# Order of the x and z column chunks in a hybrid decoder layer's input projection

## The reference, cut to what matters

```python
proj = rmsnorm(h, norm1_w) @ w_in               # q, k, v, z, xbc, dt, ga, gs
xbc = silu(causal_dwconv(xbc, conv_w, conv_b))  # 4 taps over positions; xs: 2048 columns, b and c: 512 each
y = ssd_chunked(xs, dt, a_log, bm, cm, d_skip)
y = y * silu(z)                                  # z: 2048 columns
yg = group_norm(y, 4 groups) * ssd_norm_w
h = h + ((gate_a * (attn @ w_attn_o) + gate_s * (yg @ w_ssd_o)) @ w_out)
```

## Time and profile before

| what | value |
| --- | --- |
| median of 3 runs | 1051.18 us |
| the runs | 1048.21, 1051.68, 1051.18 us |
| the profiled execution | 1048.02 us |
| its span, first to last instruction | 1046.3 us |
| PE busy | 1020.7 us (98%), 4991 matmuls |
| VectorE busy | 637.7 us (61%) |
| ScalarE busy | 467.2 us (45%) |
| GpSimd busy | 99.4 us (9%) |
| mean granted TensorE clock | 0.997 |

### The profile page before, as it was taken

One profiled execution on the slowest core, in us unless ns is written; L12 is line 12 of the kernel. 1 busy time (PEld: TensorE's weight loads), 2 busy tenths in 40 slices (PEclk: granted clock), 3 DMA queues, 4 the chain that ended last, 5 costly groups with the idle time before them and its releaser, 6 DMA issues.

```text
span 1046.3 us, 13313 instructions
## 1 busy us (share of the span) xinstructions
PE 1020.7 (98%) x4991; PEld 833.2 (80%) x4991; DVE 637.7 (61%) x915; ACT 467.2 (45%) x859; POOL 99.4 (9%) x132
## 2 busy tenths in 40 slices
PE   6999999999999989999999999999999999999997
PEld 6877777777888778778888888898888888888886
DVE  4537998795475685795663543557666666651323
ACT  6235656453555544557652322445443444431132
POOL 3001111110222110112230110000000000000000
PEclk9999999999999999999999999999999999999999
DMA  7622122224556333454444643132323223232212
GB/s 227 127 86 81 56 67 81 81 81 121 148 126 170 93 110 102 130 141 142 121 137 155 222 151 131 54 108 81 108 92 120 80 80 114 74 134 99 91 71 81
DMA packets 123641, 117.01 MB, mean 112 GB/s; under 512 B 21357, under 2 KB 111797, under 8 KB 123589
## 3 DMA queue, kind: packets, MB, share of 16 engines
q1 hardware_dynamic: 95653, 95.26, 29.4%
q10 hardware_dynamic: 25344, 12.59, 5.2%
q0 software_dynamic: 2592, 8.46, 2.3%
HBM read 109.93 MB, written 6.36 MB: 111 GB/s over the span
## 4 chain that ended last, share of the span: by engine, by line
PE 76%; DVE 12%; issue 7%; ACT 3%; POOL 1%; DMA 1%; ACTq 0%; DVEq 0%; SPq 0%; POOLq 0%
PE banks L1175 24%; PE banks L1177 23%; PE banks L1176 23%; DVE w_lo L830 2%; DVE conv_acc L1123 2%; PE banks L1273 1%; ACT decay L651 1%; PE banks L1221 1%; PE banks L1241 1%; ACT probs L608 1%; DMA x_nat<-in_x 1%; PE banks L1188 1%; DVE small L906 1%; DVE scores L903 1%; PE banks L1261 0%
## 5 line engine op out<-in xcount | busy, mean ns | idle before, releaser
L830 DVE TENSOR_TENSOR w_lo<-w_raw,w_hi 128x1024 fp32r<-128x1024 f32 (+1 forms) x166 | 199.6, 1242 | 112.1 <-ACT w_hi L574 110.7
L574 ACT ACTIVATE w_hi<-w_raw 128x1024 fp32r<-128x1024 f32 (+1 forms) x170 | 166.7, 1029 | 112.4 <-PE banks L1177 107.6
L1175 PE MATMUL banks<-xn_hi,w_hi 128*128 128x512 f32 x528 | 212.9, 403 | 0.7 <-DVE w_lo L830 0.5
L1176 PE MATMUL banks<-xn_lo,w_hi 128*128 128x512 f32 x528 | 206.7, 391 | 0.0
L1177 PE MATMUL banks<-xn_hi,w_lo 128*128 128x512 f32 x528 | 206.6, 391 | 0.0
L1175 PE MATMUL banks<-hn_hi,w_hi 128*128 128x512 f32 (+1 forms) x384 | 142.8, 372 | 0.0
L1176 PE MATMUL banks<-hn_lo,w_hi 128*128 128x512 f32 (+1 forms) x384 | 142.6, 371 | 0.0
L1177 PE MATMUL banks<-hn_hi,w_lo 128*128 128x512 f32 (+1 forms) x384 | 142.6, 371 | 0.0
L1175 PEld LDWEIGHTS banks<-xn_hi,w_hi 128*128 128x128 f32 x528 | 99.6, 189 | 31.3 <-issue 11.2
L1177 PEld LDWEIGHTS banks<-xn_hi,w_lo 128*128 128x128 f32 x528 | 99.4, 188 | 21.8
L1176 PEld LDWEIGHTS banks<-xn_lo,w_hi 128*128 128x128 f32 x528 | 99.7, 189 | 19.0
(11 more groups left out here) (204 smaller groups left out, 1456.1 us busy)
## 6 DMA issues: line engine op xcount, KB each, us to landing
w_raw<-in_w_in SPq DMA_DIRECT2D x29, 1024.0 KB, 5.5
w_raw<-in_w_up SPq DMA_DIRECT2D x22, 1024.0 KB, 5.1
decay<-acs_scratch ACTq DMA_DIRECT2D x16, 512.0 KB, 6.3
w_raw<-in_w_ssd_o SPq DMA_DIRECT2D x8, 1024.0 KB, 6.0
w_raw<-in_w_down SPq DMA_DIRECT2D x8, 1024.0 KB, 5.0
w_raw<-in_w_in SPq DMA_DIRECT2D x16, 256.0 KB, 4.6
w_raw<-in_w_attn_o SPq DMA_DIRECT2D x16, 256.0 KB, 4.7
decay_off<-acs_scratch ACTq DMA_DIRECT2D x32, 128.0 KB, 3.5
```

Of the source, the lines that this page charges most:

```text
L574: A.activation(whi[:, c % 2, lo_:hi_], raw[:, c % 2, lo_:hi_], ACT.Copy).then_inc(w_rounded, 1)
L830: V.tensor_tensor(wlo[:, c % 2, lo_:hi_], raw[:, c % 2, lo_:hi_], f32(whi[:, c % 2, lo_:hi_]), ALU.subtract).then_inc(w_split, 1)
L1175: T.matmul(out_, w[0], m[0], start=first, stop=False)
L1176: T.matmul(out_, w[0], m[1], start=False, stop=False)
```

## The change

The same chunks in another order, in both stretches. Every x chunk is followed by the z chunk of the same number. The number of chunks is the same, ga 0 and xs 6 stay where they are in the list, and so do all rides. In the second stretch the kinds of s1 to s16 by chunk were xs 4, xs 5, z 4, z 5, xs 6, xs 7, z 6, z 7. They become xs 4, z 4, xs 5, z 5, xs 6, z 6, xs 7, z 7.

```diff
 CHUNKS += [("bc", i) for i in range(4)]
-CHUNKS += [("xs", 0), ("xs", 1), ("z", 0), ("z", 1), ("xs", 2), ("xs", 3), ("z", 2), ("z", 3)]
+for _i in range(4):
+    CHUNKS += [("xs", _i), ("z", _i)]
 for _i in range(4):
     CHUNKS += [("ga", _i), ("ao", _i)]
-CHUNKS += [("xs", 4), ("xs", 5), ("z", 4), ("z", 5), ("xs", 6), ("xs", 7), ("z", 6), ("z", 7)]
+for _i in range(4, 8):
+    CHUNKS += [("xs", _i), ("z", _i)]
 CHUNKS += [("gs", i) for i in range(4)]
```

## The result

| what | before | after |
| --- | --- | --- |
| median of 20 runs each, in turn on one chip | 1049.38 us | 1051.88 us |
| the runs | 1047.97 to 1051.68 us | 1051.39 to 1053.36 us |
| the profiled execution | 1048.02 us | 1051.48 us |
| its span | 1046.3 us | 1049.7 us |
| its mean granted clock | 0.997 | 0.995 |

The ratio of after to before is 1.0026, with a 95% interval of 1.0019 to 1.0032. The change makes the kernel 2.5 us slower, by less than the 0.3% that the prediction called no difference. The three runs of before that stood ahead of the prediction are the first three of the 20. Their median was 1.8 us above that of all 20.

The account below looks back on a forecast made before the run. TensorE, busy 1020.7 of 1046.3 us, was taken as the bound, so order only moves its waits. Terms -0.5 + 0 + 1.0 - 1.3 + 1.4 + 1.7 = +2.3 us on a 1051.18 us median gave 1053.5 us, range 1049.2 to 1057.0.

Parts of the forecast that it names:

- 1, first stretch: First stretch: the wait at 188 us for a bank eviction goes, -0.5 us.
- 2, s2 and s3: s2 and s3: the 2.50 us wait for the sum of squares and the clock fall behind it stay, 0 us.
- 3, wait in s10: s5 to s10: step 8's and 9's loads go out later, so the wait in s10 grows to 2.8 us, +1.0 us.
- 4, s13: s11 to s13: taps move away, so the 0.95 us wait for the scaled x goes, -1.3 us.
- 5, s15: s14 and s15: step 11's decay product falls behind the taps, a new TensorE wait, +1.4 us.
- 6, s16: Behind s16: the second copy's load, late behind the tanh, delays the sum of features, +1.7 us.
- rival (a): Clock falls once more behind s10's longer wait: 1.7 us on top, +4.0 us, 1055.2 us; chance 0.26.
- the bound of +2.4: Upper bound for the s10 wait's growth, if the second load is not issued until the rounding is done: +2.4 us.
- rival (b): Delays add up in s9 to s11 and behind s16: +4.5 to +6 us, 1056.2 us; chance 0.12.
- (c): Evening out works, no new waits in s10, s15 or behind s16: -1.8 us, 1049.4 us; chance 0.12.
- (d): The waits of s2 and their clock fall go too: -6.0 us, 1045.2 us; chance 0.06.
- (e): Nothing happens, since rides set the pace and evictions were hidden: 0 us, 1051.2 us; chance 0.09.

Follow-up runs that it names:

- first_only: Kernel before with the new chunk order in the first stretch alone: 1048.2 us, ratio 0.9987.
- xs67_only: Kernel before with only xs 7 and z 6 swapped in the second stretch: 1051.0 us, ratio 1.0015.
- copy11_early: Changed kernel with ScalarE's load of step 11's second copy two slots earlier, in slot 0 of s14: 1052.34 us, ratio 1.0023 to before.
- decay8_early: Changed kernel with VectorE's decay product of step 8 one slot earlier, ahead of the split: 1050.31 us, ratio 1.0007 to before.
- before_again: Kernel before, unchanged, profiled once more: 1050.07 us.
- sums_later: Changed kernel with TensorE's sums over features of groups 1 and 2 half a unit later: 1045.18 us, ratio 0.9953 to before.
- decay11_ahead: Changed kernel with VectorE's decay product of step 11 ahead of the taps of s14: 1054.34 us, ratio 1.0042 to before.
- all_new_order: Changed kernel with four moves: decay products of steps 8 and 11 and step 11's second copy earlier, two sums later: 1043.88 us, ratio 0.9941.

## Why the prediction was right, and where it wasn't

The sign, the size of the sum and the places of the waits were right. The steps that led to the waits in s10 and behind s16 were right only in part. Point by point, by the profiles:

| part | forecast | measured |
| --- | --- | --- |
| 1, first stretch | -0.5 | -0.47, alone in first_only |
| 2, s2 and s3 | 0 | 0.0 |
| 3, wait in s10 | +1.0 | +0.86, and a fall of the clock, +1.55 |
| 4, s13 | -1.3 | -1.53 (-1.52 in xs67_only) |
| 5, s15 | +1.4 | +1.50 |
| 6, s16 | +1.7 | +1.29 |
| sum | +2.3 | +1.7 without the fall, +3.2 with it |

**The waits** came to 1.7 us where I had summed 2.3. The rest of the measured +2.5 fits the clock. The mean clock of after's 20 runs is 0.995 in the median, that of the runs of before beside the experiments 0.996, and a thousandth of 1049 us is 1.0 us. At 1.55 us a fall that is 0.5 to 0.7 falls more in a run of after. This is an estimate from the means; only the profiled executions show where the clock fell. That sum and median agree to 0.2 us is partly luck: two smaller terms made up for a fall that the forecast had left to rival (a).

**The base** was off by 1.8 us, the sum by 0.2. 1053.5 us is the median of three runs plus 2.3. Of the two levels that the three runs showed, the lower one, with the profiled execution, was the nearer to the median of 20.

**Part 3** had the times right, but by luck. The load left at 410.75 and 418.30 us (forecast 411.2 and 418.6), the second while the rounding of 418.18 still ran, so the bound of +2.4 did not come into play, nor rival (b). L943 ran at 417.87 and 424.19 (forecast 418.1 to 418.4, and 424.6). But the load was not what held L943 up. In after the trace gives 5.3 and 5.6 us from issue to landing, where before had 6.9 and 5.9. So the loads were there at 416.1 and 423.9, and ScalarE read the first at 417.14 (L646). VectorE came to both L943 straight from the group_norm ride (L885, rows at 417.26 and 423.58), which in s6 stands behind the unit's taps and SiLU. The forecast carried the 6.9 us over and left that work of VectorE in s6 out; the two errors met at nearly the same time. From there some 0.9 us of delay run through to the decay product, as forecast.

**Part 5** had TensorE 0.5 us early at the group in s15, where parts 1, 3 and 4 add up to -0.8 us, and left VectorE's chain at its old times. With the fall taken off, TensorE was there at 475.6 instead of 476.1 us and the product was done at 477.0 instead of 477.55. Both were half a us early, so the wait came out.

**Part 6** is the term that was mis-sized, the wait 1.02 instead of 1.7 us. With the 1.55 us of the fall taken off, the load went out at 475.9 and was served at 480.0, so it was 0.6 us early against the forecast of 476.5 and took 4.0 instead of 4.6 us. What then ended last was not the load but VectorE's split (L832), behind the rounding that ScalarE began 0.76 us late because it was still issuing. The gated y began at 480.7 on that scale, and TensorE came 0.4 us earlier than I had it. The split ended only 0.1 us behind the copied load (482.30 against 482.14 us in after), so the two were nearly level. The 0.4 us were a slip in the working: parts 1, 3, 4 and 5 add up to +0.6 us, which puts TensorE at 484.6 and not 485.0 (in before it begins that sum at 484.00 us without a wait). It came at 484.63 on that scale. With the slip mended the forecast of part 6 would have been +2.1, further off.

**Rival (a)** came about in the profile and in size: +1.55 us for a second fall, 1.7 named. Its condition, "it decides from a wait of some 2.5 us", is no sharp bound, but it came near. Counted over all 14 profiles from 60 us on, the clock fell behind 14 of the 15 waits of 2.46 us and more, and behind 3 of the 51 between 0.94 and 2.25 us. The exceptions are the wait of 2.69 us in copy11_early, behind which it stayed up, and those of 1.01 us (decay8_early), 1.02 us (xs67_only) and 1.82 us (before_again). Behind the waits of 2.7 us in s10 it fell in 4 profiles of 5, so the 0.26 given to this rival was low. The window of copy11_early around s10's wait:

```profile
434.00:440.00 6.00, 4.14 (x33) 3.57 (x34) 5.23 (x8) 1.42 (x3) 0.00 (x0) 1.00 0.79 238
```

That of sums_later around the same wait:

```profile
430.00:436.00 6.00, 5.66 (x33) 4.83 (x34) 5.02 (x8) 1.42 (x3) 0.00 (x0) 0.72 0.76 208
```

Behind waits of the same 2.69 us the clock is at 1.00 in one and at 0.72 in the other. The Trainium skill, TensorE: Matmul & The Clock Gate, Part 1, has the gate watch activity on a schedule of its own, and tells of one kernel whose number of slow matmuls at its start changed from run to run. The two profiles of before agree with it for a fall in mid-kernel: one program, waits of 1.84 and 1.82 us, a fall behind the second alone. But the coin that the prediction drew from that rule was worse than its bound of some 2.5 us: the long waits were nearly always followed by a fall, the short ones seldom.

**Rivals (c), (d) and (e)** fell. The waits in s15 and behind s16 are there. decay11_ahead takes the first away by removing its cause, and the second grows; copy11_early takes the second away, but by making the first longer. s2 is as before. sums_later gives in s2 what (d) would have given, 4.3 us in the profile, but by another edit.

Left open: what share the load and VectorE's chain have in the wait behind s16, and whether the new order could be ahead of the old one with rides placed anew from the start. all_new_order moves four of them.

## What to carry to other kernels

Evening out an engine's load over the chunks can cost more than it gives where the rides between them were placed for the old order: a slot came to lie behind 2.3 us of taps when its unit became an x unit. The wait in s15 hung on that, and by the timelines the one behind s16 hung on the same taps. Where VectorE is busy for most of a unit, as in s11 of decay8_early, much of a wait taken from TensorE in one ride can come back in the next. When a forecast time comes true, look at what ended the wait before taking the reason for shown. Look first for a short TensorE operation whose input comes from a long chain and put it half a unit later: with the clock that it kept up it was worth more than the whole reordering, in either order.

## What the runs showed of the hardware

- A pause of TensorE of 1.0 us or more, in a stream that is busy 97% of the time, can cost the pause and another 1.5 to 1.6 us for one fall of the clock. Behind waits of 2.46 to 3.06 us it fell 14 times of 15, behind those of 0.94 to 2.25 us 3 times of 51. Whether it does can change from run to run of one program (waits of 1.84 and 1.82 us in the two profiles of before). This is part of why the 20 runs of before lie between 1047.97 and 1051.68 us: of the runs beside the experiments, those at a mean clock of 0.997 took 1048.5 us in the mean, those at 0.995 1050.0. In copy11_early and decay11_ahead the stretch at the lower clock behind s2 lasted longer and cost 1.6 us more (55.59 us from the group in s1 to L1263 in s10, where after has 53.98).
- ScalarE issues its two DMAs in 1.27 us, beside an activation of 0.63 us that starts at the same time, and the next activation starts 0.69 to 0.76 us late (rows at 477.47 and 478.85 of after, 469.67 and 470.99 of copy11_early). In copy11_early the load that was moved ahead was paid for by what stood behind it: the wait in s15 grew by 0.8 us.
- The same kind of load, 512 KB of decay rows issued by ScalarE, took 6.9 and 5.9 us from issue to landing in before (issued at 408.98 and 417.27) and 5.3 and 5.6 us in after (410.75 and 418.30). A landing time read from one place of a trace need not hold when the load is issued 1.8 us later.
